# Decoder trunk on one core: softmax weights scaled before the transposes instead of after the value product

## The reference

```
def masked_softmax(logits, valid, sink=None):
    ...
    e = jnp.exp(logits - m)
    den = jnp.sum(e, axis=-1, keepdims=True)
    if sink is not None:
        den = den + jnp.exp(sink - m)
    return e / jnp.where(den > 0, den, 1.0)
...
def b_finish(x, o_cmp, o_sel, o_win, z, gl, gate, w_out):
    ob = jnp.stack([o_cmp, o_sel, o_win], axis=2).reshape(n, t, N_BRANCH, N_HEADS, HEAD_DIM)
    mix = jnp.sum(jax.nn.sigmoid(gl)[..., None] * ob * jax.nn.silu(z), axis=2)
    return x + gate * (mix.reshape(n, t, HD) @ w_out)
```

## Time and profile before

| | |
|---|---|
| median of 3 runs | 1699.21 us (1693.39 to 1700.59) |
| profiled execution: span, first to last instruction | 1699.8 us |
| mean granted clock of TensorE | 0.966 |
| phase a, pairs | about 118 to 454 us of the span |
| phase b, pairs | about 752 to 1581 us of the span |
| busy: PE, PEld, DVE, ACT, POOL | 1588.0, 1425.7, 934.7, 613.7, 485.8 us |

### The profile page before, as it was taken

One profiled execution on the slowest core, in us unless ns is written; L12 is line 12 of the kernel. 1 busy time (PEld: TensorE's weight loads), 2 busy tenths in 40 slices (PEclk: granted clock), 3 DMA queues, 4 the chain that ended last, 5 costly groups with the idle time before them and its releaser, 6 DMA issues.

```text
span 1699.8 us, 31847 instructions
## 1 busy us (share of the span) xinstructions
PE 1588.0 (93%) x11936; PEld 1425.7 (84%) x11936; DVE 934.7 (55%) x2396; ACT 613.7 (36%) x1356; POOL 485.8 (29%) x294
## 2 busy tenths in 40 slices
PE   4579999999699997899999999999999999998997
PEld 1478888888599997788998989989899898886897
DVE  3635555555645415555555755657556575578556
ACT  3413333333214414224434344344443444444112
POOL 0232412221841315355121121211212112149661
PEclk9689999999799997999999999999999999999999
DMA  9233333232612134501021130211101111033732
GB/s 329 92 92 106 106 106 106 107 106 88 236 67 75 47 136 124 141 26 35 15 64 35 29 84 17 88 35 29 35 17 38 35 29 35 18 84 104 255 145 100
DMA packets 82594, 145.16 MB, mean 85 GB/s; under 512 B 19170, under 2 KB 54146, under 8 KB 82274
## 3 DMA queue, kind: packets, MB, share of 16 engines
q1 hardware_dynamic: 69210, 128.64, 23.1%
q10 hardware_dynamic: 10288, 8.46, 1.6%
q0 software_dynamic: 2944, 6.04, 1.3%
HBM read 128.96 MB, written 19.35 MB: 87 GB/s over the span
## 4 chain that ended last, share of the span: by engine, by line
PE 86%; DVE 4%; DMA 3%; ACT 3%; issue 2%; SPq 2%; ACTq 0%; DVEq 0%
PE PS L1032 15%; PE PS L1034 15%; PE PS L1033 15%; PE PS L1287 11%; PE PS L1300 10%; PE PS L1267 5%; PE PS L1268 4%; PE PS L1406 2%; PE PS L1277 2%; DMA WR<-w_ada 2%; PE PS L1229 1%; DMA WR<-sw_v 1%; PE PS L1296 1%; PE PS L1249 1%; PE PS L1382 1%
## 5 line engine op out<-in xcount | busy, mean ns | idle before, releaser
L1032 PE MATMUL PS<-HT_r,WR_r 128*128 128x344 f32 x1344 | 448.8, 334 | 20.0 <-DVE XT_r L1823 15.3
L1034 PE MATMUL PS<-HT_r,WR_r 128*128 128x344 f32 x1344 | 433.4, 322 | 0.0
L1033 PE MATMUL PS<-XT_r,WR_r 128*128 128x344 f32 x1344 | 433.2, 322 | 0.0
L669 POOL TENSOR_TENSOR WR_r<-WR,ONE 128x1024 fp32r<-128x1024 f32 x60 | 116.6, 1943 | 1042.6 <-DMA WR<-w_b 598.3
L1631 ACT ACTIVATE PB<-PB,NM 128x257 f32<-128x257 f32 (+9 forms) x384 | 248.8, 650 | 171.4 <-DVE NM L2023 171.1
L1032 PEld LDWEIGHTS PS<-HT_r,WR_r 128*128 128x128 f32 x1344 | 257.2, 191 | 22.9 <-issue 19.9
L1033 PEld LDWEIGHTS PS<-XT_r,WR_r 128*128 128x128 f32 x1344 | 257.1, 191 | 0.0
L1034 PEld LDWEIGHTS PS<-HT_r,WR_r 128*128 128x128 f32 x1344 | 256.5, 191 | 0.0
L2036 DVE COPY PT<-PS 128x256 f32<-128x256 f32 (+2 forms) x192 | 121.6, 633 | 211.8 <-PE PS L1287 210.7
L1287 PE MATMUL PS<-CST,PB 128*128 128x128 f32 (+1 forms) x1360 | 226.5, 286 | 0.9 <-ACT PT L1639 0.9
L1300 PE MATMUL PS<-PT,VT 128*64 128x128 f32 x2592 | 204.0, 285 | 6.0 <-DVE PT L2036 2.8
(11 more groups left out here) (310 smaller groups left out, 2389.5 us busy)
## 6 DMA issues: line engine op xcount, KB each, us to landing
WR<-w_ada SPq DMA_DIRECT2D x64, 512.0 KB, 5.4
WR<-w_b SPq DMA_DIRECT2D x32, 512.0 KB, 3.3
WR<-w_a SPq DMA_DIRECT2D x17, 512.0 KB, 4.4
STR<-scratch SPq DMA_DIRECT2D x128, 48.0 KB, 1.9
XT<-x SPq DMA_DIRECT2D x8, 516.0 KB, 9.1
HT<-x SPq DMA_DIRECT2D x8, 516.0 KB, 7.2
HT<-x_mid SPq DMA_DIRECT2D x8, 516.0 KB, 5.0
STR<-scratch SPq DMA_DIRECT2D x128, 32.0 KB, 1.9
```

Source lines behind the costliest of these rows:

```text
L669: pool.tensor_tensor(high_r, raw, ONE[:, 0:1].unsqueeze(2).to_broadcast([P, NC, P]), ALU.mult).then_inc(sem("w_split"), 1)
L1032: pe.matmul(out, hw[:, k, :], high, start=(k == 0), stop=False)
L1033: pe.matmul(out, hw[:, k, :], low, start=False, stop=False)
L1034: return pe.matmul(out, lw[:, k, :], high, start=False, stop=(k == NC - 1))
```

## The change

The factor of a row is applied to the weights before they are transposed. After the two exponentials of a unit, DVE takes 1/DEN for the two heads and, in phase b, multiplies it by the sigmoid gate (step `dv`); ACT multiplies each head's weights in PB in place by it (step `sc`). The cmp unit's block is normalised by DVE alone (step `cn`). The transposes of the row factors, their widening (`rg`) and the multiply that read them (`t1`) are gone; `oe` multiplies the half's result by the SiLU gate directly. Waits on `t1` elsewhere become waits on `oe` or `b_mix`.

```diff
+    def weights_of(un):
+
+        for x in un["parts"]:
+            emit("ex", x)
+        if un["b"] != "cmp":
+            emit("dv", un)
+            for x in un["parts"]:
+                emit("sc", x)
+
+    weights_of(units[0])
+    pending = []
...
     def flush():
-        if late:
-            emit("tr", late)
-            emit("t1", late)
         for g in pending:
             emit("pv", g)
...
                 flush()
                 emit("sm", nxt["parts"][1])
-                emit("rg", ending[0])
+                emit("cn", un)
             if early_fill:
-                for x in nxt["parts"]:
-                    emit("ex", x)
+                weights_of(nxt)
                 fill(here)
...
-        for hf in ending[0:1] if un["b"] != "cmp" else []:
-            emit("rg", hf)
         emit("tr", gs[0])
         emit("ev", gs[0])
         if nxt and not to_cmp and not early_fill:
-            for x in nxt["parts"]:
-                emit("ex", x)
+            weights_of(nxt)
         if not early_fill:
             fill(here)
         leaving = [fl for fl, k0, k1, end in here if end]
         if un["b"] == "cmp":
-            emit("tr", ending[0])
-            emit("t1", ending[0])
...
-        if un["b"] == "cmp":
-            emit("rg", ending[1])
-            late = ending[1]
-        elif ending:
-            emit("tr", ending[0])
-            emit("t1", ending[0])
...
+                        un = x["unit"]
+                        if un["b"] == "cmp":
+                            pe.wait_ge(sem("b_cn"), un["it"] + 1)
                         else:
-                            pe.wait_ge(sem(ph + "_ex"), un["parts"][-1]["x"] + 1)
+                            pe.wait_ge(sem(ph + "_sc"), un["parts"][-1]["y"] + 1)
...
+                    elif what == "sc":
+                        un, s = x["unit"], x["s"]
+                        p_ = PB[:, un["slot"] + s, un["at"]:un["at"] + un["keys"]]
+                        act.wait_ge(sem(ph + "_dv"), x["y"] // 2 + 1)
+                        act.activation(p_, p_, ACT.Copy, scale=RG[:, x["y"] // 2 % 2, s:s + 1]).then_inc(sem(ph + "_sc"), 1)
...
+                    elif what == "dv":
+                        y = x["parts"][0]["y"] // 2
+                        rg, den = RG[:, y % 2, :], DEN[:, BR[x["b"]], :, x["qb"]]
+                        dve.wait_ge(sem(ph + "_ex"), x["parts"][-1]["x"] + 1)
                         if ph == "a":
+                            dve.reciprocal(rg, den).then_inc(sem(ph + "_dv"), 1)
                         else:
+                            c0 = BR[x["b"]] * H + 2 * x["it"]
+                            step(dve.reciprocal(rg, den))
+                            dve.tensor_tensor(rg, rg, SG[:, x["qb"], c0:c0 + 2], ALU.mult).then_inc(sem(ph + "_dv"), 1)
+                    elif what == "cn":
+                        dve.wait_ge(sem(ph + "_ex"), x["parts"][-1]["x"] + 1)
+                        x3 = PB[:, x["slot"], x["at"]:x["at"] + x["keys"]].rearrange("p (q c) -> p q c", c=NCB)
+                        den, c0 = NM[:, 4, :], 2 * x["it"]
+                        den2 = den.rearrange("p (q s) -> p q s", s=2)
+                        step(dve.tensor_reduce(den, x3, AX, ALU.add))
+                        step(dve.tensor_scalar(den, den, 1.0 / BIG, None, ALU.max))
+                        step(dve.reciprocal(den, den))
+                        step(dve.tensor_tensor(den2, den2, SG[:, :, c0:c0 + 2], ALU.mult))
+                        dve.tensor_tensor(x3, x3, den.unsqueeze(2).to_broadcast([P, 2 * QB, NCB]), ALU.mult).then_inc(sem("b_cn"), 1)
...
-                        dve.wait_ge(sem(ph + "_t1"), h + 1)
+                        dve.wait_ge(sem("fill_ev"), gate_done(ph, b, it, half))
                         if b in ("a", "cmp"):
...
-                            dve.tensor_tensor(out, PS[:, 6, :], SS[:, :], ALU.mult).then_inc(sem(ph + "_oe"), 1)
+                            dve.scalar_tensor_tensor(out, PS[:, 6, :], 0.5, gate, ALU.mult, ALU.mult).then_inc(sem(ph + "_oe"), 1)
```

## The result

The changed kernel takes 1773.95 us (median of 4 runs, 1765.91 to 1779.53) where the kernel before, run beside it, takes 1699.01: a ratio of 1.043, 95% interval 1.040 to 1.046. The forecast had the direction right and the size wrong: 33 us were expected, 75 came, and the time lies outside the range. The profiled execution has a span of 1777.8 us.

The account below looks back on a forecast made before the run. The prediction took TensorE, busy 93% of the span, to bound the kernel: 1699.8 + 22 (seven pairs) + 9 (last pair) + 0 (phase a) = 1731, taken as 1732 us, range 1704 to 1760.

Parts of the forecast that it names:

- Removed: Row-factor transposes gone: 1.45 us at four places plus 0.53 at cmp, 2.0 us saved per steady pair.
- The mechanism: ScalarE's later evictions wait behind VectorE's step and two copies, VectorE's behind the reciprocal; TensorE waits for both before value products.
- Place A: Turn of unit 7, next unit 1024 columns: ScalarE's eviction ends 21.15, TensorE asked at 19.60, stall 1.55 us.
- The sum of the stalls: Per steady pair, 1.55+2.1+0.45+0.25+0.4+0.4 = 5.15 us; minus 2.0 removed gives +3.15, +22 over seven pairs.
- Cmp: Normalisation ahead of cmp's transposes, unit 1's copies ahead of tanhs and first eviction: 0.4 us lost, nothing saved.
- Place B: Turn of unit 13, where delays accumulate: eviction ends 56.62, TensorE asked at 54.52, stall 2.1 us.
- The clock: Rival, 0.14: TensorE's clock also falls after waits, each costing half of some 3 us, 13 us more: 1745.
- The smaller places: Stalls of 0.45 us in the turn of 9; estimates of 0.25 and 0.4 in turns of 5 and 14.
- The upper bound, 1.1: Upper price of VectorE's reciprocal and product, taken as 0.40 us; from a 32-column instruction behind a reciprocal, 0.89.
- The length is not the point; the place is: ScalarE has 63 idle us per pair and the copies take 20; their place in its in-order queue decides.
- Phase a, 0: Sixteen factor groups saved (5.8 us) against waits of about 0.5 per pair and 2 in the last: together nothing.
- Last pair, +9: From unit 3 on no fill covers the longer chain; TensorE ends up 9.5 us late at unit 16; taken as +9.

Follow-up runs that it names:

- removal_only: The changed kernel without the whole normalisation (no reciprocal, product, scaling copies or cmp normalisation); 1663.31 us, ratio to the kernel before 0.979.
- no_round_trip: The changed kernel with copies that scale by ones and do not wait for VectorE, which still makes reciprocal and product; 1731.97 us, 1.018.
- busy_in_place_b: The changed kernel with seven more TensorE products of constants per pair, in the two waits of the turn of unit 13; 1775.64 us, 1.044.
- no_product: The changed kernel without the gate of sel and win, so the factor is the reciprocal alone; 1751.38 us, 1.030.
- gate_as_scalar: The changed kernel with reciprocal and product made per part, the product taking the gate as a per-row operand instead of a second tensor; 1730.55 us, 1.020.
- half_copies: The changed kernel without the scaling of the second half of each part's columns, waits and orders kept; 1735.94 us, 1.021.
- late_scale: The changed kernel with reciprocal, product and both copies issued behind the evictions of their turn; 1797.16 us, 1.058.
- copies_last: The changed kernel with only ScalarE's two copies issued behind the evictions, reciprocal and product staying right behind the exponentials; 1758.71 us, 1.035.
- copies_only: The changed kernel without VectorE's step and cmp's normalisation; the copies scale by ones and wait for the second exponential; 1720.52 us, 1.013.
- vector_only: The changed kernel without ScalarE's scaling copies; VectorE still makes reciprocal and product and normalises cmp; 1695.10 us, 0.997.

## Why the prediction was right in direction and wrong in size

**Removed: right, and a little small.** 2.0 us a pair forecast, 2.7 measured. Most of the difference is cmp's first factor group, where the forecast counted nothing as saved: from cmp's first transposes to its value products it took 1.84 us before, and it takes 1.28 in removal_only.

**The mechanism: right.** Evictions of both engines stand behind reciprocal and copies, and TensorE waits for them in the turns named. The prices of two copies up to the hand-over (1.44, measured 1.46: 1083.84 to 1085.30) and of an undisturbed VectorE step (0.40, measured 0.43) held. Place A came out by luck: 1.55 was forecast for ScalarE's eviction alone; TensorE waits 0.53 for VectorE's, which the sum for A did not have, and 1.02 for ScalarE's, and what follows comes 1.70 later. The sum's last step adds a microsecond without a reason (1731 taken as 1732).

**The sum of the stalls, 5.15 us per pair, is the step that failed: a steady pair takes 9.5 us more than one of removal_only (112.7 against 103.2).** The order of TensorE's instructions is the same in both, so the difference can be followed from turn to turn. What the sum had too small or did not have:

- *Cmp.* It was put at 0.4, with the eviction as its only wait. TensorE waits 0.94 for the normalisation at the transposes and 1.03 for ScalarE's eviction behind them, and is 1.9 later than in removal_only (1.3 later than in the kernel before). In no_round_trip the second wait is down to the 0.24 of removal_only and the first stays (0.6 to 1.4): ScalarE's eviction stood behind copies that waited for VectorE.
- *Place B.* It took 3.0 (2.1 forecast), since the output add, VectorE's eviction and ScalarE's all came late, one after another (0.37, 1.11 and 0.93).
- *The clock.* It was a rival of 0.14, set aside because products break the stalls of place B. Its price was right (1.5 us each, measured 1.46), its chance was not: one fall in each of the six steady pairs of the changed kernel, four behind place B and two behind place A. busy_in_place_b shows that the waits of place B bring the four. Behind unit 14, where I had a stall of 0.4, TensorE does not wait in these four pairs: the 1.3 us lost there are the slower clock.
- *The smaller places.* The turn of 9 took 0.7 (0.45 forecast), that of 5 took 0.4 (0.25), and two waits that I had not named, ahead of cmp and in the turn of 6, up to 0.4 and 0.25.
- *The VectorE step beside GpSimd.* I took 0.40 everywhere. The upper bound, 1.1, came from a 32-column instruction that took 0.89; I read it as a property of the instruction. In that trace it ended at 1551.73, and a GpSimd instruction that was running ended at 1551.69. In the changed kernel the step took up to 2.3 us in the first pair and 2.0 in the turn before place A. no_product and gate_as_scalar show 18 to 23 us for it, most of them in the first and the last pair.

Of the 47 us by which the span missed its forecast (78 against 31), some 22 lie in the six steady pairs, 9 in the first, which was counted like the steady ones, 9 in the last and 7 in phase a.

**"The length is not the point; the place is": wrong as put.** half_copies gives 38 us back for the length, and late_scale and copies_last show no place that costs nothing. The 63 us that ScalarE was idle in a pair before were room only in part: in copies_only 20 us of copies make a steady pair 4.5 us longer than in removal_only. ScalarE's waits in one steady pair of the kernel before (us in total, times, longest):

```profile
ACT PT L1639 <- PE PS L1287: 31.2, 17, 4.0
ACT PB L1631 <- DVE NM L2023: 12.7, 10, 4.1
ACT WR L1603 <- PE PS L1034: 9.4, 6, 2.5
```

Half of the idle time lies ahead of the evictions, where ScalarE waits for transposes; the rest ahead of exponentials and tanhs. The copies were in the way of the evictions in one of the places tried, and late for the next transposes in the other.

**Phase a, 0: wrong.** It took 7.2 us longer; the removal there is worth 10.3 (5.8 forecast), what is added costs 17.5 (5.5 forecast), of which 8.1 is the wait for VectorE (no_round_trip) and the rest the copies: vector_only's phase a equals removal_only's. **Last pair, +9: half.** It took 18.3; with no fills to cover, copies (11.6 over the removal) and VectorE's step (14.0) each cost most of what they cost together (17.4), and the clock there was 0.88.

That the granted clock falls after some waits at place A or B and not after others in the same place (three pairs of copies_only against three) stays open. So does how much of the 42 us of the round trip is GpSimd's hold and how much the 0.43 us themselves: gate_as_scalar, which takes the hold away, has the step per part as well, and no_product leaves out the whole instruction. Why the one-column form with a per-row operand was never held, and wider ones were, stays open too.

## What to carry to other kernels

Idle time of an in-order engine is room only if it lies between the moment the new work can start and the next thing that someone waits for; look for that gap in the timeline before counting the idle time, and if the gap is missing at one place, it may be missing at the next, as it was here. A wait handed from one engine to a second and back costs more than its two small instructions: make the factor of the first half while the second half is still being made, and keep the small product in a form that did not wait for the neighbour, as the one-column form with a per-row operand here. Where one phase of a kernel differs in sizes and cover, try a change in that phase alone: here it turned a loss of 4% into a gain of half a per cent.

## What the runs showed of the hardware that was not expected

- A VectorE product of two columns, 0.16 us alone, took up to 2.16 us beside GpSimd, one of a single column up to 2.38; each that took over 0.3 us (25 and 47 of them) ended within 0.06 us of a GpSimd instruction. With one tensor and a per-row operand the single column took 0.212 to 0.217 in all 256 cases, but the same form at 512 columns, 0.47 to 0.49 alone, took 2.69.
- TensorE's granted clock fell to the 1.2 GHz level behind places where it had waited 1.55 us (A) or 2.4 us (B), each in two or three pieces of an otherwise full pair, for some 3 us. Seven products of constants per pair in the waits of place B left no fall there, and two pairs of six fell at place A.
- An fp32 product of 128x128 by 128 columns is recorded as two instructions of 0.288 us, a transpose of the same tile as one; in place of the transposes such products kept TensorE busy 16.5 us longer per pair.
